# Sample states and sample outputs in row halves and column groups of TensorE

## The reference

```
S_t = diag(alpha_t) S_{t-1} + k_t^T v_t
o_t = q_t S_t
```

## Time and profile before

| | |
|---|---|
| median of 3 runs | 1132.45 us |
| profiled execution | 1126.76 us |
| its span, first to last instruction | 1125.0 us |
| PE busy | 1079.3 us (96%) |
| DVE, ACT, POOL busy | 516.1, 409.9, 458.4 us |
| mean granted TensorE clock | 0.987 of full speed |

### The profile page before, as it was taken

One profiled execution on the slowest core, in us unless ns is written; L12 is line 12 of the kernel. 1 busy time (PEld: TensorE's weight loads), 2 busy tenths in 40 slices (PEclk: granted clock), 3 DMA queues, 4 the chain that ended last, 5 costly groups with the idle time before them and its releaser, 6 DMA issues.

```text
span 1125.0 us, 17227 instructions
## 1 busy us (share of the span) xinstructions
PE 1079.3 (96%) x6961; PEld 965.3 (86%) x6961; DVE 516.1 (46%) x681; ACT 409.9 (36%) x588; POOL 458.4 (41%) x206
## 2 busy tenths in 40 slices
PE   3779999999999999899999999999999999999998
PEld 2449878999999999789988887999999999888886
DVE  4541000646677777434423747655445544400204
ACT  6532423333444444333334334433333333211312
POOL 2113243637767667533315302443334333334330
PEclk9879999999999999999999999999999999999999
DMA  9528644898767863686743501233223322222212
GB/s 352 102 41 103 141 112 75 91 103 149 129 121 128 125 132 39 100 66 144 134 113 104 196 1 57 76 94 93 75 80 88 93 75 84 84 75 75 92 66 84
DMA packets 137479, 115.07 MB, mean 102 GB/s; under 512 B 4777, under 2 KB 117185, under 8 KB 136401
## 3 DMA queue, kind: packets, MB, share of 16 engines
q1 hardware_dynamic: 137329, 114.25, 47.7%
q10 hardware_dynamic: 96, 0.04, 0.0%
HBM read 106.92 MB, written 7.35 MB: 102 GB/s over the span
## 4 chain that ended last, share of the span: by engine, by line
PE 72%; issue 16%; POOL 7%; DVE 2%; ACT 1%; DMA 1%; POOLq 0%; DVEq 0%; ACTq 0%
PE pair L1412 43%; PE pair L1452 11%; PE pair L1696 5%; POOL w_lo L694 3%; POOL w_lo L686 3%; PE pair L1497 2%; PE pair L1360 2%; PE pair L1603 1%; PE pair L1591 1%; DMA raw<-in_w_in 1%; PE pair L1564 1%; PE pair L1658 1%; PE pair L1575 1%; PE pair L1615 1%; DVE o_tok L1230 0%
## 5 line engine op out<-in xcount | busy, mean ns | idle before, releaser
L686 POOL TENSOR_TENSOR w_lo<-raw,w_hi 128x1024 fp32r<-128x1024 f32 x102 | 253.5, 2488 | 513.4 <-ACT w_hi L743 513.3
L1412 PE MATMUL pair<-h_hi,w_hi 128*128 128x288 f32 x1600 | 351.2, 298 | 6.9 <-DVE h_lo L1054 6.0
L1412 PE MATMUL pair<-h_hi,w_lo 128*128 128x288 f32 x1600 | 345.7, 294 | 0.0
L1412 PE MATMUL pair<-h_lo,w_hi 128*128 128x288 f32 x1600 | 345.6, 294 | 0.0
L1412 PEld LDWEIGHTS pair<-h_hi,w_hi 128*128 128x128 f32 x1600 | 259.8, 188 | 23.8 <-issue 7.5
L1412 PEld LDWEIGHTS pair<-h_lo,w_hi 128*128 128x128 f32 x1600 | 258.5, 189 | 0.0
L1412 PEld LDWEIGHTS pair<-h_hi,w_lo 128*128 128x128 f32 x1600 | 258.4, 188 | 0.0
L743 ACT ACTIVATE w_hi<-raw 128x1024 fp32r<-128x1024 f32 x118 | 123.7, 1056 | 174.2 <-PE pair L1446 91.5
L694 POOL TENSOR_TENSOR w_lo<-raw_c,w_hi 128x1024 fp32r<-128x1024 f32 x48 | 125.4, 2629 | 55.3 <-ACT w_hi L743 55.3
L743 ACT ACTIVATE w_hi<-raw_c 128x1024 fp32r<-128x1024 f32 x48 | 50.7, 1057 | 93.2 <-PE pair L1412 67.3
L398 DVE SCALAR_TENSOR_TENSOR cv<-ext,ffp,cv 128x592 f32<-128x592 f32 x44 | 82.0, 1863 | 5.7 <-DVE cv L395 3.0
(11 more groups left out here) (268 smaller groups left out, 1347.7 us busy)
## 6 DMA issues: line engine op xcount, KB each, us to landing
raw<-in_w_up SPq DMA_DIRECT2D x44, 512.0 KB, 3.7
raw<-in_w_in SPq DMA_DIRECT2D x40, 512.0 KB, 8.3
raw_c<-in_w_in SPq DMA_DIRECT2D x24, 512.0 KB, 9.4
raw_c<-in_w_ada SPq DMA_DIRECT2D x24, 512.0 KB, 8.2
raw<-in_w_down SPq DMA_DIRECT2D x22, 512.0 KB, 3.5
ada_first<-in_w_ada SPq DMA_DIRECT2D x8, 1024.0 KB, 13.5
raw<-in_w_ada SPq DMA_DIRECT2D x8, 512.0 KB, 5.1
s_in<-in_state_gla SPq DMA_DIRECT2D x8, 512.0 KB, 5.6
```

The lines of the kernel that those rows point to most:

```text
L686: pool.tensor_tensor(lo, raw[r % 2][:, :], hi.bitcast(F32), ALU.subtract).then_inc(S("w_lo_done"), 1)
L1412: ins = pe.matmul(bank[pair][:, half, 0:HALF], w[:, i, :], x[:, i, HALF * half:HALF * half + HALF], start=i == 0 and p == 0, stop=i == KT ...
```

## The change

The samples' keys and values now stand on both halves of the partitions (tokens on 0 to 63 and again on 64 to 127), so that the matmuls of `sample_deltas` for odd samples use rows 64 to 127 of TensorE and those for even samples rows 0 to 63; consecutive ones write to different PSUM banks. The matmuls of `sample_outputs` take 32 columns of weights in place of 64 and go to four column groups: even samples to output partitions 0 to 31 (samples 0 to 3) and 32 to 63 (4 to 7), odd ones to 64 to 95 and 96 to 127. The two partial sums are added: ACT copies the upper half into a new tile `os_up`, and DVE adds it to the lower half, where ACT alone had copied the outputs before. There are two more copies of values and one more of keys for each head on ACT. `k_own` is written as 128 x 512 in place of 64 x 1024, and `q_own` is cleared as 128 x 320 in place of 128 x 576. The tile `ones` and its memset go; `own` gets one more select and an addition at the start. The semaphores `x_rstd`, `o_rstd`, `y_rstd`, `x1_rstd` and `f_rstd` become one, `rstd`, with offsets in the counts; all of them are raised and awaited by DVE alone.

```diff
+    def delta_at(s):
+        return bank[3][:, s % 2, DV * (s // 2):DV * (s // 2) + DV]
...
@@ POOL
-                pool.wait_ge(S("k_tok_done"), 2 * h + 2)
+                pool.wait_ge(S("k_tok_done"), 3 * h + 3)
...
-                pool.tensor_tensor(k_own[:, :, :], k_tok[0:64, NCH, :].rearrange("p (o d) -> p o d", o=1)
-                                   .to_broadcast([64, NS, DK]), spread(own[:, :], DK), ALU.mult).then_inc(S("k_own"), 1)
+                pool.tensor_tensor(k_own[:, :, :], k_tok[:, NCH, :].rearrange("p (o d) -> p o d", o=1)
+                                   .to_broadcast([P, NS // 2, DK]), spread(own[:, 2, :], DK), ALU.mult).then_inc(S("k_own"), 1)
@@ ACT, values
                         act.activation(v_tok[0:m, t, 512 * c:512 * c + 512], one_bank((TT * c + t) % 8)[0:m, :], ACT.Copy) \
                            .then_inc(S("v_done"), 1)
+                        if t == NCH:
+                            act.activation(v_tok[64:P, t, 512 * c:512 * c + 512], one_bank((TT * c + t) % 8)[0:m, :], ACT.Copy) \
+                               .then_inc(S("v_done"), 1)
@@ ACT, heads
                 act.activation(k_tok[0:64, NCH, :], bank[2][0:64, 1, 0:DK], ACT.Copy).then_inc(S("k_tok_done"), 1)
+                act.activation(k_tok[64:P, NCH, :], bank[2][0:64, 1, 0:DK], ACT.Copy).then_inc(S("k_tok_done"), 1)
...
                     if c == NCH:
                         act.wait_ge(S("os_mm"), h + 1)
-                        act.activation(o_tok[0:64, NCH, :], bank[2][0:64, 0, 0:DV], ACT.Copy).then_inc(S("o_done"), 1)
+                        act.activation(os_up[:, :], bank[2][64:P, 0, 0:DV], ACT.Copy).then_inc(S("os_up"), 1)
                         act.wait_ge(S("o_done"), 2 * h + 2)
@@ DVE, heads
+                dve.wait_ge(S("os_up"), h + 1)
+                dve.tensor_tensor(o_tok[0:64, NCH, :], bank[2][0:64, 0, 0:DV], os_up[:, :], ALU.add).then_inc(S("o_done"), 1)
                 sample_states(2 * h)
                 silu(1)
                 sample_states(2 * h + 1)
@@ PE
-            pe.wait_ge(S("v_done"), 2 * TT)
+            pe.wait_ge(S("v_done"), 2 * (TT + 1))
...
-                dst = bank[2][0:64, 0, 0:DV]
-                pe.matmul(dst, score[0:64, HEADS * NCH + h, 0:64], v_tok[0:64, 4, DV * h:DV * h + DV], start=True, stop=False)
-                for s in range(NS):
-                    u = 2 * h + s // 4
-                    if s % 4 == 0:
-                        pe.wait_ge(S(f"s_in{u % 3}"), 16 * (u // 3 + 1))
-                    ins = pe.matmul(dst, q_own[:, 64 * s:64 * s + 64], s_in[u % 3][:, s % 4, :],
-                                    start=False, stop=s == NS - 1)
+                dst = bank[2][:, 0, 0:DV]
+                pe.matmul(dst[0:64, :], score[0:64, HEADS * NCH + h, 0:64], v_tok[0:64, 4, DV * h:DV * h + DV],
+                          start=True, stop=False)
+                for u in (2 * h, 2 * h + 1):
+                    pe.wait_ge(S(f"s_in{u % 3}"), 16 * (u // 3 + 1))
+                for s in range(4):
+                    for g in range(2):
+                        at_ = 64 * (s % 2) + 32 * g
+                        cols = 32 * (4 * g + s + g)
+                        ins = pe.matmul(dst[at_:at_ + 32, :], q_own[:, cols:cols + 32], s_in[(2 * h + g) % 3][:, s, :],
+                                        start=s == 1, stop=s >= 2)
                 ins.then_inc(S("os_mm"), 1)
...
-                    ins = pe.matmul(flat(3)[:, DV * s:DV * s + DV], k_own[:, 4 * g + s, :],
-                                    v_tok[0:64, 4, DV * h:DV * h + DV], start=True, stop=True)
+                    side = slice(64 * (s % 2), 64 * (s % 2) + 64)
+                    ins = pe.matmul(delta_at(s), k_own[side, 2 * g + s // 2, :], v_tok[side, 4, DV * h:DV * h + DV],
+                                    start=True, stop=True)
                 ins.then_inc(S("ds_mm"), 1)
```

More of the change, by code:

```diff
@@ L76 @@
 LAST = (4, 0, 1, 2, 3)
+RSTD_O = 5
+RSTD_X1 = RSTD_O + 2 * HEADS
+RSTD_F = RSTD_X1 + 2 * TT
 WO_SLOT = [None, None, 0, 1, 2, None, None, 3]
@@ L123, in layer_program @@
     o_tok = place("o_tok", [P, TT, DV], offset=g_at + 88064)
-    k_own = place("k_own", [NS * TS, NS, DK], offset=g_at + 93184)
+    k_own = place("k_own", [P, NS // 2, DK], offset=g_at + 93184)
     sq_o = place("sq_o", [P, DV], offset=g_at + 97280)
@@ L133, in layer_program @@
     k_tok = place("k_tok", [P, TT, DK], offset=g_at + 27648)
-    q_own = place("q_own", [P, NS * (NS * TS + TS)], offset=g_at + 30208)
+    q_own = place("q_own", [P, NS * (32 + TS)], offset=g_at + 30208)
+    os_up = place("os_up", [NS * TS, DV], offset=g_at + 31488)
     s_in = [place(f"s_in{i}", [P, 4, DV], offset=g_at + 36864 + 4096 * i) for i in range(3)]
@@ L180, in layer_program @@
     ident = place("ident", [P, P])
-    ones = place("ones", [P, P])
     mask = place("mask", [P, 7, 64])
-    own = place("own", [NS * TS, NS])
+    own = place("own", [P, 3, NS // 2])
     mul1 = place("mul1", [P, KT, 9])
@@ L467, in y_part @@
         dve.wait_ge(S("y_root"), t + 1)
-        dve.reciprocal(st_y[0:m, 2, t:t + 1], st_y[0:m, 1, t:t + 1]).then_inc(S("y_rstd"), 1)
-        dve.wait_ge(S("y_rstd"), t + 1)
+        dve.reciprocal(st_y[0:m, 2, t:t + 1], st_y[0:m, 1, t:t + 1]).then_inc(S("rstd"), 1)
+        dve.wait_ge(S("rstd"), RSTD_X1 + 2 * t + 1)
         if t > 0:
@@ L479, in xn_part @@
         dve.wait_ge(S("x1_root"), t + 1)
-        dve.reciprocal(st_h[0:m, 2, t:t + 1], st_h[0:m, 1, t:t + 1]).then_inc(S("x1_rstd"), 1)
-        dve.wait_ge(S("x1_rstd"), t + 1)
+        dve.reciprocal(st_h[0:m, 2, t:t + 1], st_h[0:m, 1, t:t + 1]).then_inc(S("rstd"), 1)
+        dve.wait_ge(S("rstd"), RSTD_X1 + 2 * t + 2)
         if t > 0:
@@ L661, in _ @@
             pool.memset(mask[:, :, :], 1.0).then_inc(S("p_set"), 1)
-            pool.memset(own[:, :], 1.0).then_inc(S("p_set"), 1)
-            pool.memset(ones[:, :], 1.0).then_inc(S("p_set"), 1)
+            pool.memset(own[:, :, :], 1.0).then_inc(S("p_set"), 1)
             pool.memset(eps[:, :], EPS).then_inc(S("p_set"), 1)
             pool.memset(one[:, :], 1.0).then_inc(S("p_set"), 1)
-            pool.wait_ge(S("p_set"), 6)
+            pool.wait_ge(S("p_set"), 5)
             pool.affine_select(out=ident[:, :], in_=ident[:, :], compare_op=ALU.not_equal, fill=1.0, base=0,
@@ L676, in _ @@
                                    pattern=[[2 * B, 64 // B], [0, B]], channel_multiplier=-1).then_inc(S("consts"), 1)
-            pool.affine_select(out=own[:, :], in_=own[:, :], compare_op=ALU.is_ge, fill=0.0, base=0,
-                               pattern=[[-TS, NS]], channel_multiplier=1).then_inc(S("p_sel"), 1)
+            sides = own[:, 0:2, :]
+            pool.affine_select(out=sides, in_=sides, compare_op=ALU.is_ge, fill=0.0, base=0,
+                               pattern=[[-72, 2], [-2 * TS, NS // 2]], channel_multiplier=1).then_inc(S("p_sel"), 1)
             pool.wait_ge(S("p_sel"), 8)
-            pool.affine_select(out=own[:, :], in_=own[:, :], compare_op=ALU.is_ge, fill=0.0, base=TS - 1,
-                               pattern=[[TS, NS]], channel_multiplier=-1).then_inc(S("consts"), 1)
+            pool.affine_select(out=sides, in_=sides, compare_op=ALU.is_ge, fill=0.0, base=TS - 1,
+                               pattern=[[72, 2], [2 * TS, NS // 2]], channel_multiplier=-1).then_inc(S("p_sel"), 1)
+            pool.wait_ge(S("p_sel"), 9)
+            pool.tensor_tensor(own[:, 2, :], own[:, 0, :], own[:, 1, :], ALU.add).then_inc(S("consts"), 1)
             def low(r, hi, lo, done):
@@ L700, in _ @@
             pool.memset(q_own[:, :], 0.0).then_inc(S("p_set"), 1)
-            pool.wait_ge(S("p_set"), 7)
+            pool.wait_ge(S("p_set"), 6)
             pool.wait_ge(S("back"), KT)
             for h in range(HEADS):
-                pool.wait_ge(S("k_tok_done"), 2 * h + 2)
+                if h == 0:
+                    pool.wait_ge(S("consts"), 9)
+                pool.wait_ge(S("k_tok_done"), 3 * h + 3)
                 if h > 0:
@@ L1555, in state_deltas @@
             def state_deltas(h):
-                pe.wait_ge(S("k_tok_done"), 2 * h + 1)
+                pe.wait_ge(S("k_tok_done"), 3 * h + 1)
                 if h == 0:
@@ L1568, in outputs @@
             def outputs(h):
-                pe.wait_ge(S("k_tok_done"), 2 * h + 2)
+                pe.wait_ge(S("k_tok_done"), 3 * h + 3)
                 pe.wait_ge(S("decayed"), 2)
```

20 lines of the change are left out of this document (10 added, 10 removed).

## The result

The changed kernel takes 1124.64 us (median of 8 runs, 1119.02 to 1127.45) where the kernel before takes 1132.72 us (8 runs beside it, 1131.53 to 1133.89). The ratio is 0.9922, with a 95% interval of 0.9898 to 0.9946: 0.8% faster.

The account below looks back on a forecast made before the run. PE, busy 96% of the span, was taken to bound the kernel. Head 0 +4.6, heads 1 and 2 -5.5, head 3 -2.4 and values +0.5 gave -2.8 us: 1132.45 to 1129.7 us, range 1126.4 to 1138.0.

Parts of the forecast that it names:

- PE's new matmuls: L1591 and L1603: n matmuls take n + 1 passes in place of 2n, saving 2.73 us for each head.
- both passes overlap across all places: Rival for L1591 and L1603: full overlap, 4.2 us saved a head, about -7.5, 1125 us; chance 0.04.
- The weight loads: In L1591's matmuls: loads of 132 to 137 ns stay hidden behind matmuls on the same rows.
- The stall in head 0: Before the second deltas: PE waits 5.0 us for DVE's states, held by `os_up` and a late weight tile.
- the prediction's 502.8: Head 0: the time in us at which PE starts its second deltas after the stall.
- The clock: Behind head 0's stall: lowered granted clock costs 2.4 us, bounds 0 and about 3.
- the clock holds: Rival for head 0: the stall comes but the clock is not lowered, -5.2, 1127.3 us; chance 0.12.
- no stall: Rival for head 0: the weight tile lands sooner, so no stall, -10.1, 1122.3 us; chance 0.08.
- The values: Before the branch A tiles: one more ACT copy of values holds PE 0.5 us longer.
- Head 3: Last head: saves 2.4 us, as normalisations beside POOL's tiles let only 0.3 of 0.63 us through.
- Branch A to head 1: Stretch through head 0: 4.6 us later than before, 2.23 from the later second deltas and 2.4 from the clock.

Follow-up runs that it names:

- both edits: Against the changed kernel: `high` late in head 0 alone, and DVE's addition behind the first four states in all heads; median 1116.23 us, ratio 0.9876 to the kernel before.

## Why the prediction was wrong

**The step that failed** is the one on PE's new matmuls, the term of 2.73 us for each head: "the two passes of one matmul follow each other in the same place and PE keeps program order, so the second pass of one matmul overlaps the first of the next, and a group of n matmuls takes n + 1 passes in place of 2n". The runs showed that passes of different places do not wait for one another. Sixteen passes on four column groups take 1.00 us, which is four times 0.216 us (the time from one pass to the next in the same place) and 0.14 us for the change of shape; eight passes on two row halves take 1.06 us, four times 0.216 and 0.19. So L1591 saves 2.60 us rather than 1.47, and L1603 0.86 rather than 0.63, twice: 4.3 us for each head in place of 2.73. The rival "both passes overlap across all places", to which I gave 0.04, was this one. I dismissed it by program order, and the same matmuls in another order show that order has next to no bearing on it: adjacent matmuls of one place cost 0.02 us. No row of before had two places at once; the rows left this open between nothing and full overlap, and I should have carried the full overlap with a chance to match. With the measured savings in the forecast's own sum, everything else as it was, it gives -2.8 - 2 x 1.58 - 1.36 - 0.23 = -7.6 us, or 1124.9 us, and the median was 1124.6 us. (1.58 is 4.31 - 2.73; in head 3 the savings ahead of the second deltas count, 3.46 - 2.10 = 1.36, and in head 0 only those of the second deltas, 0.86 - 0.63.) That these two lie so close is in part luck: the account measures -6.7 and not -7.6, since head 1 began 0.7 us later than this sum has it, and the three runs near 1120 us drew the median down. By the account alone the time would be 1132.45 - 6.7 = 1125.8 us, and also too low for the forecast's overlap.

**The weight loads stayed hidden**, as the earlier trace rows had it. The Trainium skill (TensorE: Matmul & The Clock Gate, Part 3: Packing small matmuls) says that a weight load overlaps a matmul in flight only where the row group differs. The trace disagrees with the rule. All 16 passes of the column groups use the same rows, and their 16 loads (the line L1612 in head 1: duration ns min/median/max, first and last start) together are 1.7 us, longer than the 1.00 us in which they lie. And the passes of one place follow each other every 0.216 us whether a load takes 110 ns (here), 137 ns or 187 ns:

```profile
L1612 PEld LDWEIGHTS pair<-s_in,q_own x16: 106/110/110, 538.5 to 539.0; 128*32 128x32 f32 x16
```

The same section of the Trainium skill has tiles at different places start about 4 ns apart. The trace is near that with 3.3 ns for each pass that lies between two places: 6.6 ns here, 13.3 ns in the other order.

**The stall in head 0** came where it was put, for the reason given. Moving the addition took it away, and so did moving `high`. It was 7.3, 5.5 and 6.9 us in three executions, not the 5.0 of the prediction: PE arrived earlier by its larger savings, and the landing scatters. What counts, the time of the restart, was priced by the path and not by the stall, so the larger stall cost little: PE restarted 316.0, 316.9 and 315.4 us after the first branch A tile, where the prediction's 502.8 is 315.4 us behind that tile.

**The clock** lost 2.4 us, as priced from the earlier trace rows, and 2.0 and 2.2 us in the other two executions. With the column groups alone it lost 4.0 us behind a stall of 6.2 us, more than the bound of about 3: the price was right here, its bound was not. The rivals "the clock holds" and "no stall" did not come about.

**The values** cost 0.6 us, by the wait of 1.3 us on L828, forecast 0.5.

**Head 3** saved 3.8 us where the forecast gave 2.4. Of the extra 1.4 us, nearly all is the measured overlap. PE's wait for the normalisations grew from 0.80 to 1.3 us, so 0.5 us of the 4.3 were given back there; the forecast had given back 0.33. The normalisations took 5.66 us beside POOL's tiles, against 5.46.

**Branch A to head 1** came out at +5.1, where +4.6 was forecast. With the measured saving of the second deltas the forecast's sum would be +4.4. The executions scatter here from +4.3 to +5.8, so the difference can't be laid to a cause.

**The rest.** The two parts, run alone, show what each brings: row halves 6.0 us of the stretch, column groups 0.5 us. Together they bring 7.3; the 0.8 us over the sum of the two are less than three executions of the changed kernel differ by (441.7 to 442.9). Without the stall the column groups bring their gain in head 0 too: it took 37.4 us with both edits, and 39.9 with the row halves alone. What the prediction had no term for is the pair of groups of executions, to which the rest of the gap between the medians belongs. Whether the kernel shifts their shares, or chance does with 26 runs, stays open, as does what picks the form.

## What to carry to other kernels

Matmuls that use a quarter of the columns, or half of the rows, can be put side by side in time on other columns and rows, two-pass float32 ones included; here that made 16 passes last as long as 4, whatever their order. A gain on the engine that sets the end shows where the others have no slack: before putting another engine's step ahead of what PE waits for, look at everything queued before that step, and at the first head most of all, where a late transfer makes the queue stand still. When a stall is removed, look for the next wait behind the same late transfer, and move both. And read a small gain from a stretch that leaves out what varies between executions of one kernel: here 6.2 us of the total did, nearly as much as the gain.

## What the runs showed of the hardware

- **Places of the array run side by side.** Full overlap of two-pass float32 matmuls on four column groups (3.60 to 1.00 us) and on two row halves (1.92 to 1.06), in either order; two PSUM banks in turn without the row halves bring nothing (1.92). The timeline of PE in head 1, where eight and four matmuls make one line each:

```profile
538.53 1.07 PE L1612 MATMUL pair<-s_in,q_own 128*32 128x256 f32 x16
539.53 1.13 PE L1625 MATMUL pair<-v_tok,k_own 64*128 64x256 f32 x8
```

- **A short idle can cost as much clock as a long one.** By the matmuls behind it, the idle stretch of 2.7 us cost 2.8 us of full-speed time, those of 5.5, 6.9 and 7.3 us 2.0, 2.2 and 2.4 us, and the one of 6.2 us in the run with the column groups alone 4.0. In the run with the late addition an idle of 1.3 us was followed by 0.72 of the clock, where a wait of the same length in the changed kernel was followed by 1.00.
- **A long stream of matmuls runs at one of two paces**, 130.3 or 133.5 ns for each of 1992 matmuls of 288 columns, 6.2 us in all, one or the other in each of twelve profiled executions, with either kernel and at a granted clock of 1.00 from 720 to 960 us in both.
